# Attention in query blocks of 112 rows, with stacked fp16 halves for the scores, and V turned inside the q projection

## The reference

```python
kv = rms_norm(h, kv_norm) @ w_kv            # K and V, 4 heads of 64
q = (rms_norm(h, b_norm_pre) @ w_q) / 8     # 16 heads of 64
# a real query sees the 16 meta keys and the 128 real keys that end with its own;
# a meta query sees the meta keys up to its own
s = q @ k.T, masked to -1e30
p = softmax(concat([s, sink[head]]))[..., :-1]   # one learned sink logit per head
o = p @ v
h = h + rms_norm(o @ w_o, b_norm_post)
h = h + rms_norm(conv_ffn(rms_norm(h, f_norm_pre)), f_norm_post)
```

## Time and profile before

| | |
|---|---|
| time, median of 3 runs | 2880.36 us (2878.78 to 2881.43) |
| time of the profiled execution | 2882.5 us |
| its span | 2880.5 us |
| PE busy | 2706.8 us (94%) |
| DVE busy | 1440.2 us (50%) |
| ACT busy | 942.2 us (33%) |
| POOL busy | 736.5 us (26%) |

### The profile page before, as it was taken

How to read it: one execution, slowest core, us unless ns; L and a number is a source line. 1 busy time by engine, 2 the same in 40 slices (tenths; PEclk the granted TensorE clock), 3 DMA queues, 4 the chain that set the end, 5 groups by cost and what they waited for, 6 DMA issues and landing times.

```text
span 2880.5 us, 44637 instructions
## 1 busy us (share of the span) xinstructions
PE 2706.8 (94%) x17764; PEld 1776.4 (62%) x17764; DVE 1440.2 (50%) x1763; ACT 942.2 (33%) x1729; POOL 736.5 (26%) x476
## 2 busy tenths in 40 slices
PE   7899999999997999999999789898969999999996
PEld 5566666666664666666666456454636666666664
DVE  6576767686767544455111741554175444553113
ACT  4333333343414333222111452565242233232111
POOL 1043435353253101001212410232450010011214
PEclk9999999999998999999999999899989999999998
DMA  2101101011120111111111011000101111111111
GB/s 103 44 30 37 37 30 38 30 37 35 57 87 22 51 46 48 51 51 59 51 50 45 15 37 51 1 1 1 44 15 51 49 46 51 51 54 52 49 50 59
DMA packets 37979, 123.74 MB, mean 43 GB/s; under 512 B 3312, under 2 KB 12656, under 8 KB 37872
## 3 DMA queue, kind: packets, MB, share of 16 engines
q1 hardware_dynamic: 37872, 122.25, 13.1%
HBM read 118.04 MB, written 4.19 MB: 42 GB/s over the span
## 4 chain that ended last, share of the span: by engine, by line
PE 81%; DVE 8%; ACT 5%; DVEq 2%; issue 1%; POOL 1%; POOLq 0%; ACTq 0%; DMA 0%
PE PS L1504 24%; PE PS L1505 24%; PE PS L1506 24%; PE PS L1676 2%; DVEq L1459 2%; ACT TT L989 1%; DVE UB L1075 1%; PE PS L1593 1%; DVE small L1460 1%; DVE R L1064 1%; POOL hT L524 1%; PE PS L1683 1%; PE PS L1706 1%; PE PS L1668 1%; ACT BIG L989 1%
## 5 line engine op out<-in xcount | busy, mean ns | idle before, releaser
L1504 PE MATMUL PS<-R,whi 128*128 128x384 f16 (+1 forms) x3360 | 1048.5, 312 | 29.3 <-DVE wlo L1052 18.1
L1505 PE MATMUL PS<-R,whi 128*128 128x384 f16 (+1 forms) x3360 | 1048.2, 312 | 0.0
L1506 PE MATMUL PS<-R,wlo 128*128 128x384 f16 (+1 forms) x3360 | 1048.0, 312 | 0.0
L1052 DVE SCALAR_TENSOR_TENSOR wlo<-stage,whi 128x1024 f16<-128x1024 f32 (+1 forms) x196 | 264.3, 1349 | 981.0 <-ACT whi L569 981.0
L1504 PE MATMUL PS<-BIG,whi 128*128 128x384 f16 (+1 forms) x1632 | 508.6, 312 | 10.6 <-DVE wlo L1052 8.1
L1505 PE MATMUL PS<-BIG,whi 128*128 128x384 f16 (+1 forms) x1632 | 508.5, 312 | 0.0
L1506 PE MATMUL PS<-BIG,wlo 128*128 128x384 f16 (+1 forms) x1632 | 508.4, 312 | 0.0
L1504 PEld LDWEIGHTS PS<-R,whi 128*128 128x128 f16 x3360 | 330.6, 98 | 205.9 <-issue 23.4
L1505 PEld LDWEIGHTS PS<-R,whi 128*128 128x128 f16 x3360 | 330.4, 98 | 172.6 <-issue 10.4
L1506 PEld LDWEIGHTS PS<-R,wlo 128*128 128x128 f16 x3360 | 330.5, 98 | 167.4 <-issue 2.0
L530 POOL TENSOR_TENSOR BIG<-TT,BIG 128x1040 f32 x44 | 95.0, 2159 | 854.7 <-ACT BIG L938 854.7
(11 more groups left out here) (223 smaller groups left out, 2813.7 us busy)
## 6 DMA issues: line engine op xcount, KB each, us to landing
stage<-wa SPq DMA_DIRECT2D x164, 512.0 KB, 3.5
stage<-wd SPq DMA_DIRECT2D x32, 704.0 KB, 4.0
hT<-h SPq DMA_DIRECT2D x4, 1536.0 KB, 11.4
out<-hT SPq DMA_DIRECT2D x2, 1536.0 KB, 5.8
hT<-h SPq DMA_DIRECT2D x2, 1088.0 KB, 6.4
out<-hT SPq DMA_DIRECT2D x1, 1024.0 KB, 4.7
pr<-prm SPq DMA_DIRECT2D x1, 328.0 KB, 6.4
BIG<-wdt SPq DMA_DIRECT2D x1, 128.0 KB, 10.3
```

The lines of the kernel that those rows point to most:

```text
L1052: eng.scalar_tensor_tensor(out=wlo[:, slot, 0:width], in0=stage[:, slot, 0:width], scalar=WS, in1=whi[:, slot, 0:width], op0=ALU.mult, op1 ...
L1504: eng.matmul(acc, whi[:, slot, ws], x(0, k, b), start=first, stop=False)
L1505: eng.matmul(acc, whi[:, slot, ws], x(1, k, b), start=False, stop=False)
L1506: return eng.matmul(acc, wlo[:, slot, ws], x(0, k, b), start=False, stop=last)
```

## The change

- Queries are cut into blocks of `QB` = 112 rows: nine full blocks and a tenth of 32 rows that holds the 16 meta queries and the last 16 real ones. That makes 40 units instead of 36. With 112 queries the keys of a block are 16 meta + 112 + 128 = 256, in place of 272. The first block has 128 keys, the tenth 160. 32 units are full, with 4 x 256 = 1024 columns on 112 rows.
- q is stored per head as a stack: its high half on 64 partitions and its low half on the other 64 (`q_stack`). K is stored as a high and a low tile, both repeated in the two partition halves (`k_part`). A score is then two fp16 matmuls with a contraction of 128 (the stack by K high, the stack by K low). From the third block on the keys lie in two pieces (16 meta and 240), so a head takes four matmuls, a unit 16.
- The low halves of K and q are computed by DVE from PSUM (new lines 1533 and 1546 of the changed file) after ACT's high halves: 12 operations of 64 partitions per K unit, 6 per q unit. ACT issues the high halves of a block only after DVE has done the low halves of the block before.
- V's transposes go into the q projection, one window of rows after each block. There are 18 windows (10 of own keys, 8 of previous keys), and the meta rows are copied in by POOL.
- Masks are built in three forms. The probabilities have four buffers. Scores and value products are double-buffered in PSUM. The two transposed pieces are 128 keys each, so the separate 16-row matmul of `values` and its copy (L1004) are gone. The orders of the three attention loops stay as they were.

On VectorE, in the K/V projection: the end of the first pass and the start of the second, before the change. L1052 is the low half of the weights for the third unit, L1075 and L311 prepare the q projection's input.

The core of the diff:

```diff
+QB = P - META
+NQB = (SEQ + QB - 1) // QB
+LEAD = 2
...
-        QCH = [(b, g) for b in range(NCH) for g in range(NKV)]
+        QCH = [(b, g) for b in range(NQB) for g in range(NKV)]
+        def queries(b):
+            return QB if b < NQB - 1 else 2 * META
         def keys(b):
-            return META if b == 0 else META + P if b == 1 else META + 2 * P
+            return P if b == 0 else 2 * P if b < NQB - 1 else P + 2 * META
+        V_WIN = [(QB * b, own_keys(b)) for b in range(NQB)] + [(QB * c - META, P) for c in range(1, NQB - 1)]
...
# ACT, K units
                     if i < 2:
+                        if 3 * i + b > 0:
+                            eng.wait_ge(kq_lo, 3 * i + b)
+                            eng.sem_inc(evac, 1)
                         for hh in range(2):
                             for to in range(2):
-                                kc = K2[2 * i + hh][64 * to:64 * to + 64, :].rearrange("p (c w) -> p c w", w=MW)
...
+                                r = eng.activation(k_part(0, 2 * i + hh, s, s + n)[64 * to:64 * to + 64],
+                                                   PS[64 * hh:64 * hh + 64, bank, 0:n], ACT.Copy, scale=1.0 / WS)
+                        r.then_inc(kq_hi, 1)
...
# ACT, q units
+                    for hh in range(2):
+                        r = eng.activation(q_stack(2 * i + hh, s, s + n)[64 * hh:64 * hh + 64],
+                                           PS[64 * hh:64 * hh + 64, bank, 0:n], ACT.Copy,
+                                           scale=1.0 / (WS * AD ** 0.5))
+                    r.then_inc(kq_hi, 1)
+                    if 3 * i + b > 0:
+                        eng.wait_ge(kq_lo, 6 + 3 * i + b)
+                        eng.sem_inc(evac, 1)
+                    c = 3 * i + b
+                    if c < len(V_WIN):
+                        v_copy(c)
...
# DVE, K units
+                if i < 2:
+                    for b, (s, n) in enumerate(BLK):
+                        eng.wait_ge(kq_hi, 3 * i + b + 1)
+                        for hh in range(2):
+                            own = slice(64 * hh, 64 * hh + 64)
+                            for to in range(2):
+                                r = eng.scalar_tensor_tensor(out=k_part(1, 2 * i + hh, s, s + n)[64 * to:64 * to + 64],
+                                                             in0=PS[own, 3 * i + b, 0:n], scalar=1.0 / WS,
+                                                             in1=k_part(0, 2 * i + hh, s, s + n)[own],
+                                                             op0=ALU.mult, op1=ALU.subtract)
+                        r.then_inc(kq_lo, 1)
                 split_lo(U_KV + i + 3, i % 2)
...
# TensorE
+            for i in range(KD):
+                for b in range(3):
+                    tile(U_Q + i, 3 * (J_Q + i), i % 2, i % 2, x_big, x_norm=3, blocks=(b,))
+                    if 3 * i + b < len(V_WIN):
+                        v_turn(3 * i + b)
...
             def scores(n):
-                if n > 0:
-                    eng.wait_ge(scores_masked, n)
+                if n > 1:
+                    eng.wait_ge(scores_masked, n - 1)
...
+                    for o, a, z in key_pieces(b):
+                        for part_ in range(2):
+                            m_ = eng.matmul(score_acc(n, o, o + z - a)[:, r, :], q_, k_part(part_, g, a, z),
+                                            start=(part_ == 0), stop=(part_ == 1))
...
             def out_hi(n):
                 eng.wait_ge(values_ready, n + 1)
-                eng.activation(x_out(0, n), out_t(n), ACT.Copy).then_inc(out_hi_ready, 1)
+                for o, i, a, w in out_pieces(n):
+                    r = eng.activation(x_out(0, n, i, a, w), out_t(n, o, w), ACT.Copy)
+                r.then_inc(out_hi_ready, 1)
```

More of the change, by code:

```diff
@@ new lines, in key_pieces, with v_rows, v_prev @@
+        def key_pieces(b):
+            if b == 0:
+                return [(0, 0, P)]
+            if b == 1:
+                return [(0, 0, P), (P, QB, QB + P)]
+            return [(0, 0, META), (META, QB * (b - 1), QB * (b - 1) + keys(b) - META)]
+        V_WIN = [(QB * b, own_keys(b)) for b in range(NQB)] + [(QB * c - META, P) for c in range(1, NQB - 1)]
+        def v_rows(c):
+            return V_OWN[c] if c < NQB else V_PREV[:, c - NQB, :]
+        def v_prev(b):
+            return V_OWN[0] if b == 1 else V_PREV[:, b - 2, :]
@@ L321, in probs @@
         def probs(n):
             b = QCH[n][0]
-            T = CHUNK[b][1]
-            return SM[n % 3][0:T, 0:QPK * keys(b)].rearrange("p (r w) -> p r w", r=QPK)
-        def soft(n, i):
[L327 to L333, removed]
+            T, w = queries(b), keys(b)
+            return SM[n % 4][0:T, 0:QPK * w].rearrange("p (r w) -> p r w", r=QPK)
@@ new lines, in score_acc, with out_pieces @@
+        def score_acc(n, w0, w1):
+            T = queries(QCH[n][0])
+            o = 1024 * (n % 2)
+            return PSf[0:T, o:o + 1024].rearrange("p (r w) -> p r w", r=QPK)[:, :, w0:w1]
+        def soft(n, i):
+            return small[0:queries(QCH[n][0]), n % 4, i, :]
+        def out_pieces(n):
+            b = QCH[n][0]
+            if b == NQB - 1:
+                return [(0, 0, 0, META), (META, 2, L - META, META)]
+            t0, pieces = META + QB * b, []
+            for i, (s, w) in enumerate(BLK):
+                a, z = max(t0, s), min(t0 + QB, s + w)
+                if a < z:
+                    pieces.append((a - t0, i, a, z - a))
+            return pieces
@@ L973, in _ @@
                 eng.wait_ge(v_turned, c + 1)
[L974 to L981 removed]
+                eng.activation(v_rows(c)[0:T, :], PS[0:T, 6 + c % 2, 0:256], ACT.Copy).then_inc(v_copied, 1)
@@ L1852, in transposes @@
                 for r in range(QPK):
[L1853 to L1859 removed]
+                    c = ((r % 2) * 2 + r // 2) * T
+                    if b > 0:
+                        eng.transpose(PS[:, 4, c:c + T], sm[:, r, 0:P], ident[0:T, 0:T])
+                    k0, k1 = (0, P) if b == 0 else (P, P + own_keys(b))
+                    o = eng.transpose(PS[0:own_keys(b), 5, c:c + T], sm[:, r, k0:k1], ident[0:T, 0:T])
                 o.then_inc(probs_turned, 1)
```

211 lines of the change are left out of this document (117 added, 94 removed).

## The result

The changed kernel took 2903.93 us (median of 4 runs, 2903.76 to 2905.47) against 2880.14 (4 runs, 2878.78 to 2881.43). The ratio is 1.0084, with a 95% interval of 1.0072 to 1.0096. So it is 24 us slower, where 2905 was predicted. The profiled execution took 2905.47 us with a span of 2903.7: 23.2 more than the span before, where the sum said 24.4.

What follows compares the result with a forecast made beforehand. Steady attention was taken to be bound by a loop through in-order VectorE and ACT. Start of attention +9.2, attention +14.4 and output projection +0.8 made +24.4 us, so 2905 us, range 2890 to 2922.

Steps and rivals of the forecast that it cites:

- The loop: Steady attention: VectorE and ACT in fixed order set the period, which shrinks from 6.28 to 6.03 us a unit.
- Its parts: Attention from first mask add to output projection: start, full units, split ones, clock, short steps and end sum to 234.4 us.
- The split pieces: Attention: in eight full units out_hi and out_lo are two operations each, 0.3 us a unit, 2.4 us in all.
- the 2 us for the clock at the start: Start of attention: a lower TensorE clock while it mostly waits costs 2 us (0 to 5).
- The end: Attention, from the last mask to the output projection's first matmul: 10.0 us, where it took 21.4 before.
- The K passes: K/V projection: low halves on VectorE alternate with ACT's copies, adding 4.4 us a pass, 8.8 for two (5.5 to 11).
- The overlap of ends: K/V projection: operations of one engine overlap their ends by 0.1 us each, so a pass would grow by less than 4.6.
- The rival that had them hidden: K/V projection: K low halves overlap ACT's copies, so 8.8 us falls away, giving 2896 us; chance 0.10.
- V turned: Between last V product and q projection: the 4.9 us gap falls to 0.5, -4.4; transposes inside the q projection add 4.0.
- TensorE's part: Steady attention: TensorE's work is 4.0 us in a unit of 6.03, hidden by the loop, so saving it gains nothing.
- The clock rival: Steady attention: TensorE's clock falls, its unit takes 7.0 to 8.0 us, 24 us more in all, 2929; chance 0.15.
- The fast rival: Steady attention: TensorE is the true limit, the period falls to 5.1 us, giving 2876 us; chance 0.07.

Runs made afterwards that it cites:

- e5_max_twice: The changed kernel with the maximum of every unit computed twice on VectorE: 2951.42 us.
- e3_pe_filler: The changed kernel with 12 extra unused fp16 matmuls on TensorE in all but the first two units and the last: 2903.93 us.
- e1_k_free: The changed kernel, but ACT copies all three K blocks without waiting for VectorE's low halves in between: 2896.11 us.
- e10_v16: The changed kernel with the value product of the own keys cut to 16 rows in full units: 2924.27 us, one run.
- e8_loop_cut: The changed kernel with masks two units ahead, scores three ahead, and denominators before the mask in VectorE's order: 2826.21 us.

## Why the prediction was right

**The loop** (predicted 0.25 us less a unit, 6.03): measured 6.03. e5_max_twice and e3_pe_filler show that VectorE's steps belong to it and TensorE's do not. The order was as it had been, so four more full units cost 24 us and the shorter ones and the shorter end gave back only part.

**Its parts.** The fifth mask came 12.20 us after the first (12.3 predicted). The 32 full units took 194.9 (197.4). The split pieces were mis-sized: seven of the eight units with them took 6.16, 0.13 more, not 0.3 (the eighth took 6.63, and one of the kernel before did, too). So was the 2 us for the clock at the start, which cost nothing: the second and third full units took 6.03 us at a mean clock of 0.52 and 0.63. The three short steps took 14.8 (14.7). The end took 11.5 instead of 10.0. I had followed the last unit alone through the engines. By the trace TensorE is on the path: it still has the transposes of two units and the value products of three to do, 6.5 us of work at half clock:

```profile
2029.07:2035.55 6.48, 6.47 (x40) 4.79 (x40) 1.09 (x8) 1.72 (x11) 1.24 (x1) 0.50 0.00 0
```

Together 13.4 against 14.4.

**The K passes** (8.8 predicted): from the first K copy to the start of the fourth K/V unit it took 35.0 us (1662.21 to 1697.21), before 25.2 (1662.80 to 1687.97). That is +9.8. A group of four low halves of 384 columns took 2.26 us, as L1400 had said (0.55 each). From the first K copy to the weights' low half a pass took 12.2 us (1662.21 to 1674.41), where the chain in series had been put at 11.9: VectorE's groups add up to 6.3 instead of 6.1 and the handovers to 0.3. The overlap of ends, for which I had taken 0.2 off, did not come. TensorE waited 4.8 us for the third unit's weights (4 foreseen) but 7.9, not 10, for the fourth's. Behind the first wait it ran the third unit at a mean clock of 0.78, in 13.7 us where before it took 10.8 at 1.00. The wait hid that. The rival that had them hidden is refuted, and e1_k_free shows that it could have been partly true in another order.

**V turned** (-4.4): the gap between the last V copy and the q projection fell from 4.91 to 0.55, so -4.4 as predicted. In the projection and up to the first mask add +4.7 (92.20 for 87.54), against 4.75 predicted.

**TensorE's part** was the step whose size was most wrong, and it cost nothing because the step lay off the path. I put the four value products at 2.0 us by the old time of a product; they took 0.92. The old time was that of a kernel with a separate 16-row matmul beside those of 128 rows, and e10_v16 shows that such a mix alone makes a product that slow. The scores' records span 1.44 us where I took 1.2. In sum a unit took 3.3 us, not 4.0. By the Trainium skill, page "TensorE: Matmul & The Clock Gate", section "Weight-path perf modes — Fast Weight Load (FWL) and DoubleRow", 112 columns miss the fast load, which gave an estimate of 1.5: the row lies nearer to that. The loads themselves agree with the page: at full clock a load of 112 fp16 columns (L1958) lasts 131 ns, one of 128 (L1610, in the q projection) 98. That this makes the scores as long as they are is not shown, since no run loaded 128 columns in the same place.

**The clock rival** has to be told in two halves. Its condition came true: the granted clock fell from 1.00 to 0.78 over the full units, going between the two levels unit by unit. I had argued against that from a wait of 2.13 us that stood at full clock. That was a poor row to argue from. It belongs to a unit whose value products were still those of a smaller one (144 keys), four and not six (L1876 is missing in it). Further on, a unit of the kernel before looks like this:

```profile
1897.45:1903.73 6.28, 5.75 (x35) 3.18 (x34) 3.58 (x9) 4.09 (x12) 2.00 (x1) 1.00 0.00 0
```

```profile
1903.26 0.28 PE L1855 MATMUL PS<-ident,TT 128*16 128x128 f32 x1 [0.53 <-POOL TT L553]
```

TensorE worked for 5.75 us of 6.28 and waited for 0.53, so "TensorE waits in every unit" gave a wrong picture of the slack before. After the change it waits 2.0 us a unit on average and 2.76 behind a unit at full clock, and the clock did not hold. The rival's price did not come: at half clock a unit of TensorE's takes 6.0 us, not the 7 to 8 I had doubled up, since the products were already half as long as I thought. That is just inside the loop's 6.03. e10_v16 shows how near it was: with products of the old length the same fall costs 20 us, about the 24 that the rival had. So the loop and its parts were foreseen, but that the low clock stayed free was luck: its argument claimed 2 us of slack, at half clock there were 0.04, and two errors (too slow products, too steady a clock) cancelled.

**The fast rival**, TensorE as the true limit, is refuted by e3_pe_filler and by e8_loop_cut, which changes no TensorE instruction but the lead of the scores and takes 78 us away.

## What to carry to other kernels

Where two in-order engines pass units to each other, follow the chain of waits from one unit to the same step of the next: its length is the period, and work outside it is free as long as it fits into the period at the clock that it gets. Read an engine's slack from a typical unit, not from one at the start of the stage. Before a step is moved ahead, look at what it is put in front of: the same idea (masks two ahead) gave 21 us in front of the denominators, 78 behind them, and cost 4% in the kernel before, with single buffers and the scores only two ahead.

## What the runs showed of the hardware

- Two fp32 products with 64 columns of weights, written to the two halves of the partitions, took 0.23 us each when all their matmuls hold 128 rows, and 0.52 each when 128 and 16 rows alternate, at the same clock and width (224 columns). Work on fewer rows was slower. The Trainium skill, page "TensorEngine Tiling (Array Packing)", section "Key Properties", has a rule for it: tiles of one mode work independently of each other, but a change of the tiling mode drains TensorE. Cutting one of two products to 16 rows would be such a change. The times agree with it (0.23 against 0.52 us); no run separates it from another cause.
- A weight load of 112 fp16 columns lasted longer (131 ns, L1958) than one of 128 (98 ns, L1610), both at full clock in the changed kernel.
- The granted clock between 1830 and 2000 us was 1.00 before, where TensorE waited some 0.5 us in a unit. It was 0.79 in the changed kernel, with 2.0 us of waiting, 0.95 with the extra matmuls in the units, 0.66 with the loop of 7.32 us, and 1.00 (1830 to 1900 us) in the loop of 3.77. Where TensorE's half-clock work still fits into the loop (6.0 of 6.03 us), the fall costs nothing. Where it does not (7.8 us in e10_v16), units of two lengths mix: 1.2 us more of products at full clock cost 20 us in all.
